# Post-norm decoder layer on one core: the first layer norm applied at the eviction of three up-projection slabs, x1 blocks made over 21 chunks, and x loads spaced out

## What is computed

```python
mix = jnp.einsum('bqm,md->bqd', jnp.concatenate([a, m], axis=-1), w_out)
x = layer_norm(DEEPNORM_ALPHA * x + mix, ln1_g, ln1_b)
f, conv_state = conv_ffn(x, conv_prefix, w_up, conv_w, conv_b, w_down)
x = layer_norm(DEEPNORM_ALPHA * x + f, ln2_g, ln2_b)

def layer_norm(x, g, b):
    mu = jnp.mean(xf, axis=-1, keepdims=True)
    var = jnp.mean(jnp.square(xf - mu), axis=-1, keepdims=True)
    y = (xf - mu) * lax.rsqrt(var + LN_EPS) * g + b
```

## Time and profile before

| | |
|---|---|
| median of 3 executions | 1327.71 us (1327.31 to 1328.39) |
| profiled execution | 1331.4 us, span of its trace 1329.7 us |
| TensorE busy | 1300.9 us (98%) |
| VectorE, ScalarE, GpSimd busy | 769.3, 598.5, 191.7 us (58, 45, 14%) |
| HBM traffic | 203 GB/s over the span |
| median from issue to landing of a weight chunk | 3.6 us (w_up), 6.7 us (w_out) |

### The profile page before, as it was taken

The page is one execution under the profiler, slowest core; times in us unless marked ns, Lnnn a source line. Parts: engine busy times, 40 slices in busy tenths (PEclk is TensorE's granted clock), DMA queues, the critical chain, the costliest instruction groups (busy, mean ns, idle before and its releaser), DMA issues.

```text
span 1329.7 us, 25394 instructions
## 1 busy us (share of the span) xinstructions
PE 1300.9 (98%) x9704; PEld 1212.2 (91%) x9704; DVE 769.3 (58%) x1263; ACT 598.5 (45%) x966; POOL 191.7 (14%) x303
## 2 busy tenths in 40 slices
PE   9999999999999999999999999999999999999995
PEld 9988767776669899999999999999999999999995
DVE  5657877784437686566556556556655535443434
ACT  4443332343333484464555455446455433333434
POOL 4510000013220130001001001000100500120202
PEclk9999999999999999999999999999999999999998
DMA  8868899989986355555555655555555655555552
GB/s 269 240 196 304 293 360 367 269 297 354 363 292 211 112 173 175 162 156 174 166 167 158 175 160 159 174 161 157 173 165 170 185 167 165 160 167 165 161 172 72
DMA packets 98988, 271.50 MB, mean 204 GB/s; under 512 B 13129, under 2 KB 21394, under 8 KB 98738
## 3 DMA queue, kind: packets, MB, share of 16 engines
q1 hardware_dynamic: 82978, 221.86, 54.1%
q10 hardware_dynamic: 8464, 28.88, 6.4%
q0 software_dynamic: 7424, 19.15, 4.2%
HBM read 264.66 MB, written 5.18 MB: 203 GB/s over the span
## 4 chain that ended last, share of the span: by engine, by line
PE 90%; DMA 3%; DVE 3%; SPq 1%; issue 1%; ACT 1%; ACTq 0%; DVEq 0%
PE G L487 27%; PE G L488 27%; PE G L489 26%; PE A L840 2%; DMA k_ring<-in_kT_cache 2%; PE A L655 1%; DVE w_lo L1479 1%; PE A L755 1%; SPq L315 1%; DMA raw<-in_w_out 1%; PE A L671 0%; DMA raw<-in_w_iq 0%; ACT w_hi L1123 0%; DVE z L1887 0%; PE A L768 0%
## 5 line engine op out<-in xcount | busy, mean ns | idle before, releaser
L1479 DVE TENSOR_TENSOR w_lo<-raw,w_hi 128x1024 fp32r<-128x1024 f32 x353 | 434.3, 1231 | 401.6 <-ACT w_hi L1123 400.3
L1123 ACT ACTIVATE w_hi<-raw 128x1024 fp32r<-128x1024 f32 x353 | 372.8, 1056 | 499.5 <-PE G L489 448.1
L487 PE MATMUL G<-x_hi,w_hi 128*128 128x290 f32 (+1 forms) x1856 | 557.1, 300 | 4.1 <-DVE w_lo L1479 2.0
L488 PE MATMUL G<-x_lo,w_hi 128*128 128x290 f32 (+1 forms) x1856 | 552.0, 297 | 0.0
L489 PE MATMUL G<-x_hi,w_lo 128*128 128x290 f32 (+1 forms) x1856 | 548.7, 296 | 0.0
L487 PEld LDWEIGHTS G<-x_hi,w_hi 128*128 128x128 f32 x1856 | 349.0, 188 | 12.2 <-issue 11.0
L488 PEld LDWEIGHTS G<-x_lo,w_hi 128*128 128x128 f32 x1856 | 350.8, 189 | 0.2
L489 PEld LDWEIGHTS G<-x_hi,w_lo 128*128 128x128 f32 x1856 | 348.9, 188 | 0.0
L487 PE MATMUL G<-h_hi,w_hi 128*128 128x288 f32 x704 | 208.6, 296 | 0.0
L488 PE MATMUL G<-h_lo,w_hi 128*128 128x288 f32 x704 | 207.7, 295 | 0.0
L489 PE MATMUL G<-h_hi,w_lo 128*128 128x288 f32 x704 | 207.0, 294 | 0.0
(11 more groups left out here) (321 smaller groups left out, 1137.2 us busy)
## 6 DMA issues: line engine op xcount, KB each, us to landing
raw<-in_w_up SPq DMA_DIRECT2D x176, 512.0 KB, 3.6
raw<-in_w_down SPq DMA_DIRECT2D x88, 512.0 KB, 3.6
k_ring<-in_kT_cache SPq DMA_DIRECT2D x128, 256.0 KB, 4.9
raw<-in_w_in ACTq DMA_DIRECT2D x48, 512.0 KB, 5.5
raw<-in_w_out SPq DMA_DIRECT2D x32, 512.0 KB, 6.7
v_ring_x<-in_v_cache SPq DMA_DIRECT2D x32, 256.0 KB, 5.4
v_ring_x<-in_v_cache POOLq DMA_DIRECT2D x28, 256.0 KB, 5.9
v_ring_p<-in_v_cache SPq DMA_DIRECT2D x20, 256.0 KB, 5.2
```

The source lines that it names most:

```text
L487: pe.matmul(out, hi, xh, start=start, stop=False)
L488: pe.matmul(out, hi, xl, start=False, stop=False)
L1123: act.activation(w_hi[:, c, 0:width], raw[:, c, 0:width], ACT.Copy).then_inc(hi_done, 1)
L1479: dve.tensor_tensor(w_lo[:, c, 0:width], raw[:, c, 0:width], w_hi[:, c, 0:width].bitcast(f32), ALU.subtract).then_inc(lo_done, 1)
```

## The change

The norm is y = ((z - mean) * rstd) * g + b. As it is linear for each token once mean and rstd are known, the first three up-projection slabs (`YS` = 3) now run on g*z, without mean and rstd. Two more columns, g and b, ride with the 290 columns of tokens (`NW` = 292), so that a slab also gives W'g and W'b. At eviction u = rstd * (W'(g z) - mean * W'g) + W'b.

- ScalarE and VectorE split g*z into `y_hi` and `y_lo` while the output projection runs (`scaled_high`, `scaled_low`), block by block, the last eight blocks behind its end.
- All 32 matmuls of the partial sums stand behind chunk 90 (slab 0, first chunk), and two 128x290 matmuls behind chunk 91 spread both totals over all partitions and tokens (`first_spread`). Deviation and reciprocal are then computed for 128x290 elements; `totals`, `warm` and the turning matmuls are kept only for the second norm.
- `put_norm_in` on VectorE empties the tiles of slabs 0 to 2 (two operations each), `keep_gb` on ScalarE keeps the two extra columns before, and `keep_up` adds W'b while it writes `u_ext`. The convolution of these slabs comes two chunks later than that of the others.
- The 16 blocks of x1 (needed from slab 3 on and for the residual) are made between chunks 95 and 115, as listed in `X1_AT`.
- `chunk_by_block` is not used for the up-projection any more.
- x loads go behind chunks 75, 77, 80 and 82, `kT_out` behind 79, and the conv parameters behind 84.
- The squares are kept for all 16 blocks (`sq`), the first ones one chunk later. h blocks are stored rotated by 34 (`h_block`), so that they don't lie on live data.

```diff
+YS = 3
+X1_AT = {5: (0,), 6: (1,), 7: (2, 3), 8: (4,), 9: (5,), 14: (6,), 15: (7,), 16: (8, 9), 17: (10,),
+         22: (11,), 23: (12,), 24: (13, 14), 25: (15,)}
...
@@ sync
-                if n < 79:
-                    k = 4 * (n - 75)
+                if n in (75, 77, 80, 82):
+                    k = 4 * (75, 77, 80, 82).index(n)
...
-                if n == 80:
+                if n == 79:
                     sp.wait_ge(k_roped, KVH)
                     sp.dma_start(kT_out, k_t[:]).then_inc(rows_out, 16)
+                if n == 84:
...
+                    sp.wait_ge(pa_lo, NH)
+                    sp.wait_ge(sa_lo, 1)
+                    sp.dma_start(cp_sb[:], conv_p).then_inc(late_in, 16)
+                    sp.dma_start(c_state[:], conv_ctx).then_inc(late_in, 16)
@@ tensor
+            def first_sums():
+
+                pe.wait_ge(g_free, 4 * SL_UP)
+                for g in range(4):
+                    for q in range(4):
+                        mm = pe.matmul(A[32 * q:32 * q + 32, 1, 0:NQ], ones[:, 0:32], z1q[:, 4 * g + q, :],
+                                       start=g == 0, stop=g == 3)
...
+            def first_spread():
+
+                for bank, part, kept in ((3, 3, part_a), (0, 4, part_b)):
+                    pe.wait_ge(kept, 1)
+                    pe.matmul(A[:, bank, 0:NQ], ones[:], ln_a[:, part, :], start=True, stop=True).then_inc(total_mm, 1)
...
-                    if (s, c) in SUMS:
-                        first_sums(SUMS[s, c])
-            first_sums(3)
-            totals(ln_a, NQ, 0)
-            warm(6)
...
+            for i in range(YS):
                 for c in range(8):
...
+                    if i == 0:
+                        pe.wait_ge(y_low, CK * c + CK + 1)
+                    chunk(UP0 + 8 * i + c, SL_UP + i, CK * c, 0, KB - 1, y_parts, NW)
+                    if i == 0 and c == 0:
+                        first_sums()
+                    if i == 0 and c == 1:
+                        first_spread()
@@ scalar
-                if f in (AO + 6, AO + 9, AO + 13):
-                    squares(z1q, ln_a, (f - AO - 5) // 4, SL_A, 0)
+                if f in (AO + 7, AO + 9, AO + 13):
+                    first_squares((f - AO - 5) // 4)
...
+                if f in (AO + 8, AO + 10, AO + 14):
+                    scaled_high((f - AO - 6) // 4)
...
+            act.activation(ln_a[:, 2], ln_a[:, 1], ACT.Sqrt, bias=tiny[:, 15:16]).then_inc(sd_done, 1)
+            for c in range(5, 10):
+                for k in X1_AT[c]:
+                    x1_high(k)
+                hi(UP0 + c)
@@ vector
+            for k in range(8, 12):
+                scaled_low(k)
+            lo(UP0 + 2)
+            for k in range(12, 16):
+                scaled_low(k)
+            lo(UP0 + 3)
+            dve.wait_ge(part_mm, 2)
+            dve.tensor_copy(ln_a[:, 4], A[:, 2, 0:NQ]).then_inc(part_b, 1)
+            lo(UP0 + 4)
+            dve.wait_ge(mean_kept, 1)
+            then(dve.tensor_tensor(ln_a[:, 1], ln_a[:, 0], ln_a[:, 0], ALU.mult))
+            dve.wait_ge(total_mm, 2)
+            dve.scalar_tensor_tensor(out=ln_a[:, 1], in0=A[:, 0, 0:NQ], scalar=1.0 / (32 * D), in1=ln_a[:, 1],
+                                     op0=ALU.mult, op1=ALU.subtract).then_inc(var_done, 1)
+            then(dve.tensor_tensor(z1q[:, 0], z1q[:, 0], ln_a[:, 0], ALU.subtract))
+            dve.wait_ge(sd_done, 1)
+            dve.reciprocal(A[:, 1, 0:NQ], ln_a[:, 2]).then_inc(rstd_kept, 1)
...
+            x1_next(4)
+            for c in range(5, 10):
+                x1_next(c)
+                x1_blocks(c)
+                lo(UP0 + c)
...
+            def put_norm_in(i):
+
+                if i:
+                    dve.wait_ge(gated_done, i)
+                for j in range(4):
+                    wait_tile(dve, SL_UP + i, j, UP0 + 8 * i + 7)
+                    dve.wait_ge(gb_kept, i * 4 + (j + 1))
+                    dve.scalar_tensor_tensor(out=conv[:, j, 0:NQ], in0=ln_a[:, 0], scalar=w_gb[:, j, 0:1], in1=G[:, j, 0:NQ],
+                                             op0=ALU.mult, op1=ALU.subtract).then_inc(g_free, 1)
+                for j in range(4):
+                    dve.wait_ge(g_free, i * 4 + (4 * SL_UP + j + 1))
+                    dve.tensor_tensor(conv[:, j, 0:NQ], conv[:, j, 0:NQ], A[:, 1, 0:NQ], ALU.mult).then_inc(u_ready, 1)
...
+                for c in range(10, 18):
+                    n = UP0 + 8 * i + c
+                    d = c - 10 - 2 * (i < YS)
+                    if i < YS and c == 10:
+                        put_norm_in(i)
```

More of the change, by code:

```diff
@@ L1360, in keep_shift, with first_squares @@
                 act.activation(tmp[:, 0], A[:, 0, 0:tmp.shape[2]], ACT.Copy, scale=1.0 / 128).then_inc(shift_kept, 1)
-            def squares(z, tmp, g, slab, round_):
+            def first_squares(g):
+                for k in range(4 * g, 4 * g + 4):
+                    if g == 0:
+                        act.wait_ge(shifted, k + 1)
+                    else:
+                        act.wait_ge(g_free, 4 * SL_A + k + 1)
+                    act.activation(sq[:, k], z1q[:, k], ACT.Square).then_inc(squared, 1)
@@ L1385, in norm @@
                 for k in range(KB):
[L1386 to L1393 removed]
+                    act.wait_ge(scaled, KB + k + 1)
@@ L1889, in norm @@
-                ahead = 3 if split else KB
-                for k in range(ahead):
-                    scale(k)
-                for k in range(KB if split else 0):
-                    dve.wait_ge(x1_hi, k + 1)
-                    dve.tensor_tensor(x_lo[:, k, M0:T], z[:, k], x_hi[:, k, M0:T].bitcast(f32),
-                                      ALU.subtract).then_inc(x1_lo, 1)
-                    if k + ahead < KB:
-                        scale(k + ahead)
-                    if k >= 3 and k % 2:
-                        lo(UP0 + k // 2 + 1)
+                dve.wait_ge(mean_kept, 2)
@@ L1901, in unshift_partial, with x1_rest @@
+            def x1_rest(k):
+                dve.wait_ge(x1_hi, k + 1)
+                dve.scalar_tensor_tensor(out=x_lo[:, k, M0:T], in0=z1q[:, k], scalar=ln1_sb[:, 1, k:k + 1],
+                                         in1=x_hi[:, k, M0:T].bitcast(f32), op0=ALU.add,
+                                         op1=ALU.subtract).then_inc(x1_lo, 1)
             def unshift_partial(k):
@@ new lines, in tap, with last_taps @@
+            def tap(i, j, w):
+                t = 2 * i + j % 2 + FB * (j // 2)
+                return dve.scalar_tensor_tensor(out=conv[:, j, 0:UO], in0=u_ext[:, j, w:w + UO],
+                                                scalar=cp_sb[:, t, w:w + 1], in1=conv[:, j, 0:UO],
+                                                op0=ALU.mult, op1=ALU.add)
+            def last_taps(i, j):
+                dve.wait_ge(conv_a, i * 4 + (j + 1))
+                then(tap(i, j, 1))
+                tap(i, j, 2).then_inc(conv_v, 1)
@@ new lines, in _ @@
+            for i in range(NUP):
+                for c in range(10, 18):
+                    n = UP0 + 8 * i + c
+                    d = c - 10 - 2 * (i < YS)
+                    if i < YS and c == 10:
+                        put_norm_in(i)
+                    if d == 0:
+                        last_taps(i, 0)
+                        last_taps(i, 1)
+                    if d == 1:
+                        last_taps(i, 2)
+                        last_taps(i, 3)
+                    if d == 2:
+                        gate(i)
+                    if d == 3:
+                        gate_low(i)
+                    x1_next(8 * i + c)
+                    x1_blocks(8 * i + c)
+                    if n < DN0 + 6:
+                        lo(n)
@@ L2013, in _ @@
             dve.wait_ge(g_free, 4 * (SL_DN + NDN))
-            norm(z2, ln_b, CENTRE[1], 1, False)
+            second_norm()
 def constants():
```

353 lines of the change are left out of this document (204 added, 149 removed).

## The result

| | before | after |
|---|---|---|
| median of 4 executions | 1328.05 us (1327.31 to 1330.83) | 1319.24 us (1318.55 to 1321.25) |
| profiled execution | 1331.4 us, span 1329.7 | 1318.55 us, span 1316.9 |
| first a_hi matmul to first h_hi matmul | 398.90 to 1028.05, 629.15 us | 393.81 to 1015.21, 621.40 us |
| first h_hi matmul to the end | 301.7 us | 301.7 us |

The account below looks back on a forecast made before the run. TensorE's queue was taken as the bound, busy 1300.9 of 1329.7 us. Taking out 13.97 us and adding 6.0 gave 8.0 us less, from 1327.71 to 1319.7 us, range 1318.2 to 1323.7.

Parts of the forecast that it names:

- hole of the first norm: TensorE's gap between the last output matmul and the first up-projection matmul goes: 8.12 us out.
- sums between output chunks: Partial sums standing between output-projection chunks cost TensorE 1.31 us, three times; they go: 3.93 us out.
- waits at the first two boundaries: TensorE's waits at the output projection's first two slab boundaries go by reordering x loads and squares: 0.97 and 0.95 us.
- sums in one piece: The 32 partial-sum matmuls together behind chunk 90 add 4.4 us on TensorE, at most 5.2.
- slab boundaries: TensorE's waits at seven slab boundaries and a late split on entering slab 0 add 0.4 us, bound 0 to 1.2.
- reciprocal: VectorE's reciprocal over 290 columns ahead of chunk 95 takes 2.0 us and costs TensorE nothing.
- three up-projection evictions: VectorE's new evictions of slabs 0 to 2 are 0.03 us in time, so nothing to 0.2 us each.
- The margin at chunk 95: The `lo` behind the reciprocal ends at 20.3 us, 1.1 us before TensorE reaches chunk 95 at 21.4.
- (1): Rival, chance 0.12: the reciprocal takes 6.1 us, chunk 95 waits 3.0 us; 1322.7 us, or 1323.5 with GpSimd beside it.
- (2): Rival, chance 0.08: weights come late in the output projection, TensorE waits 1 us, perhaps twice; 1321.7 us.
- (3): Rival, chance 0.05: VectorE, stretched 1.32 times beside GpSimd, becomes the bound in slabs 1 to 3; 1333.9 us.
- (4): Rival, chance 0.04: the hole only moves, about 1.0 us at each of seven boundaries; 1326.7 us, no change.

Follow-up runs that it names:

- a_no_centring: The changed kernel without GpSimd's 15 subtractions of the mean from z; first a_hi to first h_hi matmul 620.74 us, against 621.40.
- a_x1_later: The changed kernel with all 16 x1 blocks made from chunk 101 on, none in slab 0; first a_hi to first h_hi matmul 621.50 us, against 621.40.
- a_balanced: The changed kernel with x1 blocks spread, three before slab 0's end, and ScalarE's square-root table load moved; 1317.28 us against 1319.11 for the changed kernel run beside it.
- a_recip_twice: The changed kernel with a second, unused reciprocal just before the real one; first a_hi to first h_hi matmul 622.46 us, against 621.40.
- a_gather: The changed kernel with GpSimd adding up 12 of 16 blocks of z and squares, 10 sum matmuls not 32; first a_hi to first h_hi matmul 628.84 us, against 621.40.
- a_gather_later: The changed kernel with GpSimd adding up 12 blocks and x1 blocks made from chunk 101 on; first a_hi to first h_hi matmul 630.03 us, against 621.40.

## Why the prediction was right, step by step

| step | predicted, us | measured, us |
|---|---|---|
| hole of the first norm | 8.12 out | 8.12 out, 0.25 left on entering slab 0 |
| sums between output chunks | 3.93 out | 3.93 out |
| waits at the first two boundaries | 0.97 and 0.95 out | 0.96 and 0.95 (alone, on before) |
| sums in one piece | 4.4 in | 4.24 |
| spread | 0.97 in | 0.98 |
| two more columns, 576 matmuls | 0.2 in | 0.29 (133.8 ns against 133.3) |
| slab boundaries | 0.4 in | 0.25 + 0.70 + 0.03 + 0.03 = 1.01 |
| reciprocal | 2.0, hidden | 1.97, hidden |

The measured terms give 13.96 - 6.52 = 7.4 us; before also lost 0.2 us inside its slab 0, block by block, which the prediction didn't count, and which is gone. That is 7.6 of the 7.75 us; 0.1 stays unassigned. The medians give 1327.71 - 1319.24 = 8.5 us; what this has above the stretch's 7.75 is within the scatter of the whole time.

The mechanism held: the hole, the sums between chunks and the two waits went, and nothing as large came back. That the time is met to 0.5 us is in part luck. The whole time scatters by more than that, and in the stretch 0.6 us too little for the boundaries stands against 0.2 too much for the sums and 0.2 that before lost inside its slab 0 without being counted. By its own terms the range also starts at 1318.9 - 0.5 = 1318.4 and not at 1318.2, which changes nothing. Of what the prediction named as signs of being wrong one came: TensorE waited for `g_free` at the end of slab 0.

**The step that was mis-sized** is that of the three up-projection evictions: 0.03 us in time, so nothing to 0.2 us each. The evictions of slabs 1 and 2 cost 0.03 us each; that of slab 0 cost 0.70, over its bound. The prediction took the 0.03 from a boundary at which VectorE's queue had run empty in front of the eviction (the `lo` at 439.26 in before came behind 0.50 us of idle time), and asked only whether the two-part eviction is longer. Right behind the reciprocal the queue is not empty. The prediction had even listed the parts: 24 us of work in 25.6 us of slab, and stretching by GpSimd. But it counted whether the slab's work fits into the slab, and not whether the queue is empty at the one moment at which a tile must be emptied. a_no_centring removes this wait by taking GpSimd away, a_x1_later and a_balanced by moving x1 blocks.

**The margin at chunk 95** came out at about 0.3 us and not 1.1. TensorE reached the chunk at 21.5 us behind the end of the output projection (467.06 - 445.51), for 21.4 predicted, and `lo` ended at 21.1, not 20.3; from there to the matmul that it frees another 0.14 us go by (470.00 to 470.14 in a_recip_twice). The 0.8 us lie ahead of the reciprocal, which began at 15.6 and not 14.8: the split of chunk 94 was 0.3 us late, and VectorE's square of the mean took 0.96 us beside GpSimd and not 0.45. From the start of the reciprocal to the end of `lo` it was 5.5 us, as predicted. The text said that GpSimd would eat most of the margin, and it did: in a_no_centring the same `lo` ended at 20.3. a_recip_twice measures what was left.

**Rivals.** (1) The reciprocal is not long: 1.97 us, below the 2.4 us that the prediction estimated from the repeat count in the Trainium skill; the measured number decides. Above the plain pass of 0.44 us it is 5.3 ns a column, just what was read at three columns; the upper bound took the whole step between two and three columns for one column. (2) No split waited for raw beyond its time near chunk 85. (3) VectorE didn't become the bound. The prediction had stretched all of its work by 1.32, but the stretch hits only some forms. Read again, say so: beside the same centring x_lo<-z,x_hi, with two inputs from SBUF, took 585 ns, and z<-z,A, whose second input is in PSUM, 444. After shows the same: `lo` 1.72 us in place of 1.21, but the scale by A 0.94 us for two beside GpSimd (463.08) as without it (523.03 in a_x1_later), and the reciprocal 1.97 beside it and 1.98 in a_no_centring. It is `lo`, x_lo and the square of the mean that carried the delay. (4) The hole did not move.

The Trainium skill, in "SBUF — State Buffer" under "Who interferes with whom", says that a VectorE instruction with two SBUF inputs contends with a GpSimd instruction that reads SBUF, and that one with at most one SBUF input, outside the two-port modes, does not. The rows above agree. VectorE's own centring of block 0 (460.32 in after, two inputs from SBUF) took 0.47 us in the midst of GpSimd's, since the operation of GpSimd then under way had only 0.15 us to run. It also calls the contention an exclusive lock. That fits for all but the first 0.13 us: in steady alternation in a_gather a pair took 0.98 us, where 0.45 (VectorE's operation alone) + 0.80 (GpSimd's at 437.55) would be 1.25. Less 0.13 us for each of the two, about as in the rows under the result, it is 0.99.

## To carry to other kernels

When an eviction is given to an engine that also feeds the pipeline, ask what stands in that engine's queue at the moment the tile falls due, not whether the work fits into the slab; the same x1 work cost 0.7 us right ahead of the eviction and nothing when spread over other chunks. Before costing work on VectorE beside GpSimd, sort it by how many inputs it reads from SBUF: here those with one kept their time, and each of those with two waited for the end of GpSimd's operation under way, for up to 0.6 us, so that four short ones in a row took 2.5 times as long. And look for waits that a reordering alone removes before crediting a rewrite: here they were a quarter of the gain.

## What the runs showed that was not expected

- GpSimd's operations lengthened VectorE's two-input ones by nothing to 0.6 us each, by what GpSimd's had still to run and not by VectorE's own length (128x290: 0.51 us to 0.53, 0.75 and 0.96 for x_lo in after, four in a row from 1.56 to 3.92; 128x1024: 1.21 to 1.44 and 1.72). Short operations suffer most in proportion, and of a run of short ones each pays.
- Each of four waits of TensorE of 3.1 to 4.0 us was followed by 3.0 to 5.2 us at a granted clock of 0.50, that is 1.2 of 2.4 GHz (a_gather, a_gather_later). The wait of 1.7 us in a_recip_twice showed nothing beyond a restart of 0.08 us (granted clock 1.00 from 466 to 473 us).
- Making a critical operation longer can shorten the stretch elsewhere: of the 1.69 us that the second reciprocal cost, 0.70 came back, since GpSimd did more of its work while VectorE ran an operation with a single input.
- The period of the three-part matmul was 133.3 ns at 288 and at 290 columns and 133.8 at 292, but 139 at 304. The prediction's line through 290 and 304 (0.4 ns a column) gives 0.5 us for the two columns, the measured 0.29 lies between that and a floor.
